# Step sizes of a state-space scan, moved from GpSimd's scaled inputs into VectorE's masked weights

## The reference, cut to what matters

```python
cum = jnp.cumsum(dtc * a.reshape(g, e), axis=2)
seg = cum[:, :, :, None] - cum[:, :, None, :]
decay = jnp.exp(jnp.where(lower, seg, -jnp.inf))
cb = jnp.einsum("bcign,bcjgn->bcijg", cc, bc)
m = cb[..., None] * decay * dtc[:, :, None]
y_diag = jnp.einsum("bcijge,bcjgep->bcigep", m, xc)
...
y_off = jnp.einsum("bcign,bcgepn,bcige->bcigep", cc, h_in, jnp.exp(cum))
return (y_diag + y_off).reshape(bsz, l, nh, hp), h_final.reshape(bsz, nh, hp, n)
```

## Time and profile before

| | us |
|---|---|
| median of 3 runs | 2637.31 |
| lowest, highest | 2634.67, 2639.53 |
| the profiled execution, by its own time | 2638.41 |
| its span | 2636.5 |
| PE busy | 2489.4 (94%) |
| DVE busy | 1351.1 (51%) |
| ACT busy | 974.4 (37%) |
| POOL busy | 961.6 (36%) |

### The profile page before, as it was taken

How to read it: one execution, slowest core, us unless ns; L and a number is a source line. 1 busy time by engine, 2 the same in 40 slices (tenths; PEclk the granted TensorE clock), 3 DMA queues, 4 the chain that set the end, 5 groups by cost and what they waited for, 6 DMA issues and landing times.

```text
span 2636.5 us, 44461 instructions
## 1 busy us (share of the span) xinstructions
PE 2489.4 (94%) x19232; PEld 2204.0 (84%) x19232; DVE 1351.1 (51%) x2057; ACT 974.4 (37%) x1558; POOL 961.6 (36%) x553
## 2 busy tenths in 40 slices
PE   7989988999999999999999999999998988999997
PEld 5867677788887878878999999988988977989896
DVE  4646577644534644444364444466654534645453
ACT  5244453322323443334433333453332234333332
POOL 1755453344445222212445454400002214454544
PEclk9999999999999999999999999999999998999998
DMA  8432212333333211111223232322111012232321
GB/s 246 131 105 79 71 41 83 94 95 90 95 96 90 55 41 49 48 42 41 73 81 105 86 99 77 89 56 58 42 34 37 18 33 61 81 110 83 104 81 56
DMA packets 379858, 201.26 MB, mean 76 GB/s; under 512 B 6400, under 2 KB 377088, under 8 KB 379664
## 3 DMA queue, kind: packets, MB, share of 16 engines
q1 hardware_dynamic: 379664, 198.42, 26.6%
HBM read 196.30 MB, written 2.10 MB: 75 GB/s over the span
## 4 chain that ended last, share of the span: by engine, by line
PE 61%; DVE 12%; ACT 5%; issue 2%; POOL 1%; POOLq 0%; ACTq 0%; DVEq 0%
PE ps L677 48%; DVE t_ffy L2945 3%; DVE t_atq L2739 2%; ACT t_wh L645 1%; PE ps L2547 1%; PE ps L3180 1%; PE ps L2520 1%; DVE t_ffy L2948 1%; PE ps L2486 1%; PE ps L3199 1%; ACT t_ffy L2848 1%; PE ps L3203 1%; DVE t_ainv L2767 1%; DVE t_wl L655 1%; PE ps L519 1%
## 5 line engine op out<-in xcount | busy, mean ns | idle before, releaser
L655 POOL TENSOR_TENSOR t_wl<-t_raw,t_wh 128x1024 fp32r<-128x1024 f32 (+2 forms) x196 | 443.5, 2264 | 804.3 <-ACT t_wh L645 804.3
L677 PE MATMUL ps<-t_hh,t_wh 128*128 128x264 f32 (+2 forms) x1712 | 402.9, 314 | 12.1 <-DVE t_dcq L2673 3.6
L645 ACT ACTIVATE t_wh<-t_raw 128x1024 fp32r<-128x1024 f32 (+2 forms) x253 | 255.5, 1012 | 416.8 <-PE ps L677 372.1
L677 PE MATMUL ps<-t_hh,t_wl 128*128 128x264 f32 (+2 forms) x1712 | 379.2, 300 | 6.3 <-POOL t_wl L655 3.1
L677 PE MATMUL ps<-t_hl,t_wh 128*128 128x264 f32 (+2 forms) x1712 | 376.1, 301 | 0.0
L677 PEld LDWEIGHTS ps<-t_hh,t_wh 128*128 128x128 f32 x1712 | 269.9, 191 | 37.0 <-issue 19.8
L677 PEld LDWEIGHTS ps<-t_hh,t_wl 128*128 128x128 f32 x1712 | 269.5, 190 | 22.9 <-issue 6.3
L677 PEld LDWEIGHTS ps<-t_hl,t_wh 128*128 128x128 f32 x1712 | 269.1, 191 | 14.6 <-issue 7.1
L2945 DVE SCALAR_TENSOR_TENSOR t_ffy<-t_ffp,t_vec,t_ffy 128x528 f32<-128x528 f32 (+1 forms) x88 | 176.5, 2005 | 178.9 <-ACT t_ffy L2848 178.9
L655 POOL TENSOR_TENSOR t_fwl<-t_raw,t_fwh 128x1024 fp32r<-128x1024 f32 (+1 forms) x72 | 168.0, 2335 | 153.3 <-ACT t_fwh L645 153.3
L677 PE MATMUL ps<-t_fhh,t_wl 128*128 128x512 f32 (+1 forms) x704 | 211.6, 341 | 2.9 <-POOL t_wl L655 2.8
(11 more groups left out here) (571 smaller groups left out, 5429.4 us busy)
## 6 DMA issues: line engine op xcount, KB each, us to landing
t_raw<-in_up SPq DMA_DIRECT2D x44, 512.0 KB, 3.9
t_raw<-in_up2a SPq DMA_DIRECT2D x44, 512.0 KB, 3.8
t_raw<-in_up2b SPq DMA_DIRECT2D x44, 512.0 KB, 3.9
t_raw<-in_attn_in SPq DMA_DIRECT2D x33, 512.0 KB, 4.1
t_raw<-in_dn_in SPq DMA_DIRECT2D x33, 512.0 KB, 4.0
t_raw<-in_ada_w SPq DMA_DIRECT2D x32, 512.0 KB, 4.4
t_raw<-in_w_in SPq DMA_DIRECT2D x25, 512.0 KB, 4.5
t_raw<-in_down SPq DMA_DIRECT2D x16, 512.0 KB, 4.1
```

What stands on the lines that cost most here:

```text
L645: ac.activation(wh[slot_of[j]][:, 0:kc, :], raw[r % NRAW][:, 0:kc, :], ACT.Copy).then_inc(up("wh_cut", "cut", j), 1)
L655: eng.tensor_tensor(wl[slot_of[j]][:, 0:kc, :], raw[r % NRAW][:, 0:kc, :], wh[slot_of[j]][:, 0:kc, :].bitcast(F), SUB).then_inc(up(name, " ...
L677: ins = pe.matmul(ps[bank_of(j, i)][:, 0:tn], wt[slot][:, k, :], a[:, k, t0:t0 + tn], start=first, stop=last)
```

## The change

The scaled copies go: the step `x1` is no longer in the plan, GpSimd loses its eight instructions, and `yout` multiplies `xtm` itself. The step sizes are multiplied in on VectorE, in `masked`. They differ by head and by partition (token), so an instruction can take only one head: for each direction four `scalar_tensor_tensor` of 128 x 128 with a column of `dts` as the scalar stand where one `tensor_tensor` of 128 x 512 stood.

```diff
         def put_prep(u):
-            if u % 2 == 0:
-                put("x1", u // 2)
             put("prep", u, banks=3, of=8)
...
                 w.wait_ge(s.scaled, at("scaled", "masked", u, "1"))
+                w.wait_ge(s.copied, at("copied", "turn_s", c, "0"))
...
-                        pe.matmul(o, x1[c % 2][:, d, 64 * hd:64 * hd + 64], Ms[x][:, 128 * e:128 * e + 128],
+                        pe.matmul(o, xtm[:, c, 64 * hd:64 * hd + 64], Ms[x][:, 128 * e:128 * e + 128],
                                   start=d == 0, stop=False)
...
             def masked(u):
+                c, g = divmod(u, 2)
+                w.wait_ge(s.sp_done, at("sp_done", "softplus", 0))
                 w.wait_ge(s.scaled, at("scaled", "prep", u, "cb"))
...
-                    dv.tensor_tensor(four(Ms[x][:, :]), four(seg[d][:, :]),
-                                     CBm[u % 2][:, d, :].unsqueeze(1).broadcast_to([128, 4, 128]),
-                                     MUL).then_inc(up("scaled", "masked", u, str(d)), 1)
+                    for e in range(4):
+                        t, hd = slice(128 * e, 128 * e + 128), 8 * d + 4 * g + e
+                        ins = dv.scalar_tensor_tensor(out=Ms[x][:, t], in0=seg[d][:, t], scalar=dts[:, c, hd:hd + 1],
+                                                      in1=CBm[u % 2][:, d, :], op0=MUL, op1=MUL)
+                    ins.then_inc(up("scaled", "masked", u, str(d)), 1)
...
-            def x1_(c):
-                i = c % 2
-                w.wait_ge(s.copied, at("copied", "turn_s", c, "0"))
-                if c >= 2:
-                    w.wait_ge(s.weighed, at("weighed", "yout", 2 * (c - 2) + 1))
-                for d in range(2):
-                    ins = po.tensor_tensor(heads(x1[i][:, d, :]), heads(xtm[:, c, :]),
-                                           over(dts[:, c, 8 * d:8 * d + 8], 64), MUL)
-                ins.then_inc(up("pool_x", "x1", c), 1)
```

More of the change, by code:

```diff
@@ L1385, in program @@
         Hrun = vflat[:, 2048:3072].rearrange("p (d n) -> p d n", d=2)
-        x1 = [qT[:, 2 * i:2 * i + 2, :] for i in range(2)]
         cumc = sbt(sb_, "cumc", [128, 6, 16])
@@ L1420, in program @@
             "decay_s": "exped/0 exped/1", "decay_c": "exped/0 exped/1 pool_x/0 pool_x/1", "masked": "scaled/0 scaled/1",
-            "x1": "pool_x", "state": "multiplied", "run": "h_run",
+            "state": "multiplied", "run": "h_run",
             "yout": "weighed scaled/a0 scaled/a1 scaled/b",
@@ L1928, in gp_zero @@
                 po.memset(gp[1][:, :], 0.0).then_inc(up("pool_x", "gp_zero"), 1)
-            return {"mix": mix, "x1": x1_, "state": state_, "decay_c": decay_c, "mixs_low": mixs_low, "gp_zero": gp_zero}
+            return {"mix": mix, "state": state_, "decay_c": decay_c, "mixs_low": mixs_low, "gp_zero": gp_zero}
         xa = [xT[:, c, :] for c in range(KD)]
```

## The result

| | median us | runs | lowest, highest |
|---|---|---|---|
| kernel before | 2638.42 | 4 | 2634.67, 2643.32 |
| changed kernel | 2652.99 | 4 | 2651.97, 2657.28 |

The ratio is 1.0055, with a 95% interval of 1.0042 to 1.0068: slower by 11 to 18 us, where the forecast was 2649 (2639.5 to 2656) and slower. The two kernels were run a second time beside each other later, and gave 2652.34 against 2639.87, a ratio of 1.0045 (1.003 to 1.006). Of the executions behind the later tables, one of the kernel before (4767 us) and one of the kernel with an input from PSUM (13363 us) stand far outside and enter no ratio.

The account below looks back on a forecast made before the run. The scan was taken as paced by VectorE and GpSimd together, their SBUF instructions excluding each other. Terms +4.7, +4.0 and +3.2 made +11.9 us, passed on in full: 2649 us, eight in ten from 2639.5 to 2656.

Parts of the forecast that it names:

- two holds: Each steady unit: GpSimd's two t_Cs hold VectorE's seventh and eighth t_Ms, 0.96 us each, 1.92 together; likeliest case, chance 0.50.
- units 0 and 1: Start of the scan: eight pieces with two holds in each unit, +2.4 us a unit, together +4.7.
- units 2 to 5: Steady part of the scan: four units at 6.54 us, 26.2 instead of 22.2, +4.0.
- units 6 and 7: Last two units: t_Cs holds t_zs and the first t_Ms, t_ml the last; 7.4 us each, +3.2.
- tail: From the end of the last t_Ms to the last t_zs: as now, nothing added.
- Removed copies: GpSimd loses 1.04 us a unit of t_qT in the loop; worth only what it no longer holds up.
- The pieces: VectorE's masked step: eight instructions at 0.265 us, 2.12 us a unit against 1.20; bounds 0.20 to 0.385 each.
- one hold: Rival: the seventh t_Ms goes before t_Cs, only the eighth is held; +6 to +7 us, 2644, chance 0.16.
- The rival on the clock: TensorE idles 1.9 us a unit and falls to 1.2 GHz for most of the scan; +7, 2656, chance 0.10.
- Passing to the end: After the scan everything waits behind the last t_zs, so every microsecond of the scan passes on in full.
- Burst: Rival: the four small instructions go through together and GpSimd waits; +2.4 us, 2639.7, chance 0.15.
- Faster: Rival: t_Cs fits beside PSUM work, VectorE hardly held, a unit 4.62 us; -4 us, 2633, chance 0.09.

Follow-up runs that it names:

- input from PSUM: Changed kernel with the masked step reading the product of C and B from its PSUM bank, triangle mask left out: 2640.89 us, ratio 1.0002 to the kernel before.
- tiny `t_Cs`: Changed kernel with GpSimd multiplying only 8 of the 512 columns of each t_Cs, the rest left out: 2641.43 us, ratio 1.0002 to the kernel before.
- split alone: Kernel before, scaled copies kept, with the masked step as eight scalar_tensor_tensor of 128 x 128 (also called split only): 2652.78 us, ratio 1.005.
- slower ScalarE: Changed kernel with two unread exponentials more a unit on ScalarE in units 0 to 5, so t_Cs starts later: 2648.28 us, ratio 1.0031 to before.
- log version: Kernel before without copies or split, the step size's logarithm added to the bias of ScalarE's exponential: 2639.59 us, ratio 0.9997.
- fillers: Changed kernel with 16 or 10 unread matmuls of 256 columns on TensorE ahead of the last yout: 2652.38 and 2651.06 us, ratios 1.0055 and 1.0038 to before.

## Why the prediction was right, step by step

| step | forecast | measured |
|---|---|---|
| one piece, in a row of eight | 0.265 | 0.263 |
| two holds | 1.92 | 1.71 and 2.06, mean 1.88 |
| a steady unit | 6.54 | 6.48 |
| units 0 and 1 | +4.7 | +4.5 |
| units 2 to 5 | +4.0 | +3.7 |
| units 6 and 7 | +3.2 | +1.9 |
| tail | 0 | +2.1 |
| scan | +11.9 | +12.2 |
| whole, by medians | +11.7 | +14.6, then +12.5 |

- **What bounds.** Right. The scan is not bounded by an engine's own work but by VectorE's plus what GpSimd holds of it. Three experiments took the holds away by different means. With tiny `t_Cs` and with an input from PSUM none of the 64 pieces was held, and the scan was 13.6 and 12.1 us shorter; with a later `t_Cs` eight holds fewer in units 0 to 5 made it 6.2 us shorter.
- **Removed copies.** Their gain was taken as what they no longer hold up. Right: with the split in, they are worth nothing in a steady unit; alone they are worth 0.45 us a unit. The remark that the 6.54 agree with what both engines need of the shared resource, as "no accident", was wrong: the split alone has the same unit with the copies in it.
- **The pieces.** 0.265 was chosen between 0.20 and 0.385, because the row of 0.352 us for one such instruction and the overlap of 0.08 of unlinked neighbours stand in the trace. Measured 0.343 and 0.08. The Trainium skill's "VectorE: DVE Perf Modes", section on the TRN2 errata, would have given 0.19 (an estimate from its 58 + FD cycles); no run shows that for this instruction, where the step is 0.263.
- **Two holds in each unit.** Right in number and in place (the seventh and the eighth), in all of units 0 to 5. That it was two and not one hung on 0.03 us or less, which the prediction said it could not know and gave 0.50 to 0.16; the runs with the slower ScalarE show how little it takes to get one hold instead.
- **Units 6 and 7.** The mechanism was right in the main (`t_zs` and the first `t_Ms` meet `t_Cs`, the end meets `t_ml`), but I let `t_ml` hold a piece in both units. In unit 6 it came 0.02 us before the last piece (409.90 and 409.92), while the seventh still ran, and the last went first: the unit took 5.9 us instead of 7.4, unit 7 took 7.6. That is the 1.3 us by which this term was too large.
- **The tail.** This is the step that failed: "From there to the last t_zs: as now", a term put at nothing without a reason. TensorE is idle for 5.03 us, runs the last `yout` at 1.2 GHz, and its 32 matmuls take 4.6 us instead of 2.5. The rival on the clock had the mechanism, and looked for it in the steady units, where TensorE runs at 1.00 throughout and has slack; at the end of the scan nothing absorbs it. I had even written that it "may cost 1 to 2 us" behind the scan and left that out of the sum. What is shown is the price of the lower level, 2.1 us. What brings it to the last `yout` is not: the kernel with only the copies removed, with nothing split, has it after 3.16 us of idleness (tail 5.38), the log version after 3.17 does not (tail 3.79), and in both profiles of the kernel before it falls on unit 6. The two errors, +1.3 and -2.1, nearly cancel in the 11.9; that the scan came out within 0.3 us is in that part luck.
- **Passing to the end.** Assumed, and borne out within the noise. The scan was longer by 12.2 us and the median by 14.6 and 12.5; in the other runs the two changed by +14.0 and +12.7 (split only), +6.0 and +8.2 (slower ScalarE), +12.3 and +12.3, +12.6 and +11.2 (fillers), and where the scan changed by less than 3 us the median lay 0.7 to 3.2 us above what the scan says.
- **The signs.** Most came as named. TensorE's idle time is shorter than "some 2 us before each `yout`": 0.46 and 0.81 us in steady units, with 0.84 more ahead of the sums of `prep`. The last `t_zs` ended at 423.75 instead of near 421 (409.7 + 11.9 = 421.6), since the scan began 1.8 us later (365.34 against 363.53) and was 0.3 us longer than forecast.
- **The rivals.** Burst: refuted, each unit from 0 to 5 has two pieces of 1.17 to 1.41 us. Faster: its condition was that `t_Cs` starts after the eighth; slower ScalarE shows a unit in which it does (`t_Cs` at 390.22, the eighth piece 0.03 us ahead of it), with 2.19 us for eight.

The Trainium skill, "SBUF — State Buffer", section "Who interferes with whom", describes this: the instruction with two SBUF inputs and GpSimd's exclude each other for a whole instruction each. By that rule, the trace agrees, and the run with the input from PSUM is its cleanest case. That the first to start goes first has to be read with a grain, for starts as close as these don't tell: GpSimd's row is 0.03 us ahead in unit 3 (388.66 to 388.69) and 0.01 or less in unit 1 (first two rows), and goes first; it is 0.02 us ahead in unit 6 (last two rows), and VectorE's piece is not held.

```profile
375.70 1.27 POOL L1907 TENSOR_TENSOR t_Cs<-t_Cs,t_xbc 128x512 f32<-128x512 f32 x1 [4.12 <-ACT t_Cs L1662]
375.71 1.41 DVE L1780 SCALAR_TENSOR_TENSOR t_Ms<-t_seg,t_dts,t_CBm 128x128 f32<-128x128 f32 x1
...
409.90 1.74 POOL L1899 TENSOR_TENSOR t_ml<-t_vT,t_mh 128x512 fp32r<-128x512 f32 x1 [1.63 <-ACT t_mh L1626]
409.92 0.34 DVE L1780 SCALAR_TENSOR_TENSOR t_Ms<-t_seg,t_dts,t_CBm 128x128 f32<-128x128 f32 x1
```

## What to carry to other kernels

Before cutting a VectorE instruction with two SBUF inputs into pieces, look at what GpSimd starts while they run: each cut is an opening, and the piece behind it can be held for GpSimd's whole instruction (here 1.0 us for a piece of 0.26), not for a piece's. Read it from durations, not from idle time, since held instructions count as busy: compare the minimum, median and maximum of a line. And look whether an operation already takes a scalar for each partition, as the bias of an exponential does: here the step sizes went in there without copies and without a split, at no cost that the whole time shows.

## What the runs showed of the hardware

- A `scalar_tensor_tensor` of 128 x 128 with one input from PSUM and one from SBUF takes 0.341 us, with both from SBUF 0.343: the source changes nothing in the length, only whether GpSimd can hold it.
- Adding work to an engine made the changed kernel faster: 12 exponentials on ScalarE shortened its scan by 6.2 us.
- TensorE's level is not a function of the idle time just before: the last `yout` began after 3.17 us of it in two kernels, at 2.4 GHz in the log version and at 1.2 GHz in the one with the input from PSUM. The two rows, in this order (TensorE's timeline):

```profile
403.89 0.40 PE L1616 MATMUL ps<-t_Ms,t_kT 128*64 128x128 f32 x2 [3.17 <-DVE t_Ms L1786]
```

```profile
404.91 0.66 PE L1614 MATMUL ps<-t_Ms,t_kT 128*64 128x128 f32 x2 [3.17 <-DVE t_Ms L1780]
```

- Fp32 matmuls of 256 columns show as two records each and step by 0.224 us a record at 2.4 GHz (7.17 / 32).
